# Mixture-of-experts stage: ranked experts, shared passes and plain f32 products on column groups

## The reference, cut to what matters

```python
N_GROUPS, EXPERTS_PER_GROUP, TOP_K, D_EXPERT = 4, 8, 2, 512      # 32 experts
lg = t @ w_router_group + b_router_group
g_sel = argmax(lg); g_w = softmax(lg)[g_sel]
le_sel = (t @ w_router_expert + b_router_expert)[g_sel]           # 8 logits of that group
top_v, top_i = top_k(le_sel, 2)
w_pair = g_w * softmax(top_v); e_id = g_sel * 8 + top_i
# for every expert e, over the rows routed to it:
hb = silu(xb @ w1[e]) * (xb @ w3[e])      # w1, w3: 1024 x 512
y  = (hb @ w2[e]) * w_b                    # w2: 512 x 1024
```

## Time and profile before

| | us |
|---|---|
| timed runs, median of 3 (lowest, highest) | 1218.3 (1218.05, 1220.96) |
| the profiled execution, by its span | 1219.4 |
| TensorE busy | 1147.7 (94%) |
| VectorE busy | 842.4 (69%) |
| ScalarE busy | 686.2 (56%) |
| GpSimd busy | 305.2 (25%) |
| DMA, mean over the span | 247 GB/s |

### The profile page before, as it was taken

The page is one execution under the profiler, slowest core; times in us unless marked ns, Lnnn a source line. Parts: engine busy times, 40 slices in busy tenths (PEclk is TensorE's granted clock), DMA queues, the critical chain, the costliest instruction groups (busy, mean ns, idle before and its releaser), DMA issues. The chain is left out here.

```text
span 1219.4 us, 16721 instructions
## 1 busy us (share of the span) xinstructions
PE 1147.7 (94%) x5993; PEld 921.9 (76%) x5993; DVE 842.4 (69%) x882; ACT 686.2 (56%) x799; POOL 305.2 (25%) x304
## 2 busy tenths in 40 slices
PE   4999999999888989999499999999999999999996
PEld 2677787777676878878478888888888888888873
DVE  3643232113688764616859999999999999999986
ACT  4332233223677541235257777787777777777754
POOL 1122131000113001002204334334433433443310
PEclk9999999999799999999789999999999999999988
DMA  9634534555501216421399999999999999999964
GB/s 357 216 132 147 140 124 157 181 181 181 200 1 38 85 45 234 136 70 35 134 361 384 386 377 378 380 368 370 360 372 362 362 369 368 367 363 371 363 254 172
DMA packets 151017, 301.30 MB, mean 247 GB/s; under 512 B 12031, under 2 KB 18304, under 8 KB 150322
## 3 DMA queue, kind: packets, MB, share of 16 engines
q1 hardware_dynamic: 135792, 271.07, 61.8%
q0 software_dynamic: 15008, 29.47, 7.3%
q10 hardware_dynamic: 162, 0.05, 0.0%
HBM read 290.68 MB, written 32.67 MB: 265 GB/s over the span
## 5 line engine op out<-in xcount | busy, mean ns | idle before, releaser
L1308 PE MATMUL psum<-w_hi,act_hi 128*128 128x512 f32 (+1 forms) x1248 | 497.8, 399 | 7.4 <-DVE act_lo L2205 2.4
L1310 PE MATMUL psum<-w_hi,act_lo 128*128 128x512 f32 (+1 forms) x1248 | 485.6, 389 | 0.0
L1309 PE MATMUL psum<-w_lo,act_hi 128*128 128x512 f32 (+1 forms) x1248 | 484.7, 388 | 0.0
L1308 PEld LDWEIGHTS psum<-w_hi,act_hi 128*128 128x128 f32 x1248 | 236.4, 189 | 71.4 <-issue 14.5
L1310 PEld LDWEIGHTS psum<-w_hi,act_lo 128*128 128x128 f32 x1248 | 236.2, 189 | 49.7
L1309 PEld LDWEIGHTS psum<-w_lo,act_hi 128*128 128x128 f32 x1248 | 236.8, 190 | 43.9
L2058 DVE TENSOR_TENSOR w_lo<-raw_extra,w_hi 128x2048 fp32r<-128x2048 f32 x96 | 217.2, 2290 | 35.2 <-ACT w_hi L1167 35.1
L2058 DVE TENSOR_TENSOR w_lo<-raw_mix,w_hi 128x2048 fp32r<-128x2048 f32 x96 | 219.7, 2288 | 13.4 <-ACT w_hi L1167 12.3
L1167 ACT ACTIVATE w_hi<-raw_mix 128x2048 fp32r<-128x2048 f32 x96 | 183.9, 1916 | 46.0 <-PE psum L1310 37.3
L1167 ACT ACTIVATE w_hi<-raw_extra 128x2048 fp32r<-128x2048 f32 x96 | 182.6, 1913 | 7.0 <-PE psum L1310 6.7
L1767 DVE TENSOR_TENSOR w_lo<-raw_mix,w_hi 128x2048 fp32r<-128x2048 f32 (+1 forms) x24 | 52.8, 2202 | 147.3 <-ACT w_hi L959 147.3
(11 more groups left out here) (308 smaller groups left out, 1265.6 us busy)
## 6 DMA issues: line engine op xcount, KB each, us to landing
raw_mix<-in_w_e SPq DMA_DIRECT2D x96, 1024.0 KB, 9.5
raw_extra<-in_w_e SPq DMA_DIRECT2D x96, 1024.0 KB, 9.6
raw_mix<-in_w_in SPq DMA_DIRECT2D x16, 1024.0 KB, 5.6
raw_mix<-in_w_ada SPq DMA_DIRECT2D x16, 1024.0 KB, 7.0
ada_first<-in_w_ada SPq DMA_DIRECT2D x8, 1024.0 KB, 14.4
gates_scratch<-rows POOLq DMA_DIRECT2D x20, 256.0 KB, 3.2
y_scratch<-lam SPq DMA_DIRECT2D x1, 5120.0 KB, 16.8
yrow<-gates_scratch POOLq DMA_DIRECT2D x20, 256.0 KB, 4.3
```

What stands on the lines that cost most here:

```text
L1308: pe.matmul(out, a_hi(ka_), w_hi[:, kw, :], start=s, stop=False)
L1309: pe.matmul(out, a_hi(ka_), w_lo[:, kw, :], start=False, stop=False)
L1310: ins = pe.matmul(out, a_lo(ka_), w_hi[:, kw, :], start=False, stop=e)
```

## The change

Three experts (numbers 0 to 2) and the last one (31) have fixed places. The 28 between are ranked by row count on the chip: VectorE compares each count with all others, TensorE turns the ranks into expert numbers and per-pass tables, and SyncE loads each expert number into a register ahead of its weight loads. `WIDTHS` lists 20 passes of 128 rows: 8 with one expert (three first, the four largest ranked, the last) and 12 with two of 64 rows each. Further rounds run if a count passes its place.

The split is gone from the experts. A step is two plain f32 products with 64 stationary columns, on column groups 0 to 63 and 64 to 127 of the same bank; in a pass of two experts each group has its own weights, in a pass of one both have the same. Weight loads go to 15 slots (`ring`): the three of `raw_mix`, the six of the then unused `w_hi` and `w_lo`, six over the attention rows. The k index is taken as partition-major (k = 8p + j), so that a partition's part of a unit is one run of 8 KB in DRAM (4 rows of 2 KB before); the transposes read the gathered rows at a stride of 8, the gated product at a stride of 4. A slot is free when its unit's products are done. GpSimd no longer copies table columns. The code for further rounds is new and is left out below.

```diff
-RAW_MIX, RAW_MOE, HL = 3, 6, 3
+RAW_MIX, RING, HL = 3, 15, 3
...
+LEAD, ALONE, QUADS = 3, 4, 0
+PAIRS = (NE - LEAD - 1 - ALONE - 4 * QUADS) // 2
+RANKED = NE - LEAD - 1
+WIDTHS = [1, 1, 1, 2, 2, 1, 2, 2, 2, 2, 2, 1, 2, 2, 1, 2, 1, 2, 2, 1]
...
+            first, step = {1: (0, ALONE), 2: (ALONE, PAIRS), 4: (ALONE + 2 * PAIRS, QUADS)}[n]
+            passes.append([("rank", first + x * step + i) for x in range(n)])
...
+    units = [(0, 1, 0), (0, 1, 1)]
+    for p in range(len(passes)):
+        units += [(p, 3, 0), (p, 3, 1)]
+        if p + 1 < len(passes):
+            units += [(p + 1, 1, 0), (p + 1, 1, 1)]
+        units += [(p, 2, 0), (p, 2, 1)]
+    loads = [(n, p, m, u, x) for n, (p, m, u) in enumerate(units) for x in range(len(passes[p]))]
...
-        w1 = t["w_e1"].rearrange("l e (k p) n -> (l e) p k n", p=P)
-        w3 = t["w_e3"].rearrange("l e (k p) n -> (l e) p k n", p=P)
-        w2 = t["w_e2"].rearrange("l e (k p) n -> (l e) p k n", p=P)
+        w_e = {1: t["w_e1"].rearrange("l e (p k) n -> (l e) p (k n)", p=P),
+               3: t["w_e3"].rearrange("l e (p k) n -> (l e) p (k n)", p=P),
+               2: t["w_e2"].rearrange("l e (p k) n -> (l e) p (k n)", p=P)}
...
+                _, p, m, u, x = moe_loads[j]
+                e = expert_number(*passes[p][x])
+                if j >= RING:
+                    sp.wait_ge(moe_mm, moe_loads[j - RING][0] + 1)
+                sp.dma_start(ring(j % RING), w_e[m][e][:, u * UNIT:(u + 1) * UNIT]).then_inc(raw_in[j % RING], 16)
...
+                for x in range(HL):
+                    sp.wait_ge(tile_mm, 5 * (NS - HL + x + 1))
+                    ring_load(RAW_MIX + 2 * x)
+                    ring_load(RAW_MIX + 2 * x + 1)
...
+                sp.wait_ge(h2_out, 16 * NT)
+                sp.wait_ge(h2t_done, 2 * NT)
+                for j in range(RAW_MIX + 2 * HL, len(moe_loads)):
+                    if j == RAW_MIX + 2 * HL + 4:
+                        sp.wait_ge(moe_g[0], 16)
+                    if j == RING - 1:
+                        sp.wait_ge(rt_mm, 1 + NT)
+                    ring_load(j)
...
+                if p >= 2:
+                    po.wait_ge(moe_xt, p - 1)
+                if p == LEAD:
+                    po.wait_ge(pass_done, 3)
...
+            for p in range(NP - 1):
+                if p + 2 < NP:
+                    gather(p + 2)
+                scatter(p)
...
+            def x_columns_copied(p):
+                par = p % 2
+                ac.wait_ge(moe_xt, p + 1)
+                ac.activation(expert_xT[:, par * D:(par + 1) * D], bank(0, 2), ACT.Copy).then_inc(moe_xc, 1)
...
+            pe.wait_ge(ranks_made, 2)
+            pe.matmul(bank(6)[0:1, 2 * NE:2 * NE + RANKED], tokval[0:NE, 0:1], perm[0:NE, :], start=True, stop=True)
+            pe.matmul(bank(6)[:, 0:2 * NE], ones_row[0:NE, :], excess[0:NE, :], start=True, stop=True).then_inc(ids_mm, 1)
...
+            xg_v = xg[:, :].rearrange("p (b q k) -> p b k q", b=2, k=KD)
+            gp_v = gprod[:, :].rearrange("p (q k) -> p k q", k=4)
...
+            def up_half(out, u, par, slots):
+
+                n = max(2, len(slots))
+                w = P // n
+                for kk in range(4):
+                    k = 4 * u + kk
+                    for x in range(n):
+                        a = par * D + k * P + x * w
+                        ins = pe.matmul(out[x * w:(x + 1) * w, :], expert_xT[:, a:a + w], ring(slots[x % len(slots)])[:, kk * 512:(kk + 1) * 512],
+                                        start=(k == 0), stop=(k == KD - 1))
+                return ins
+
+            def down_half(u, slots):
+                n = max(2, len(slots))
+                w = P // n
+                for kk in range(2):
+                    k = 2 * u + kk
+                    for b_ in range(2):
+                        for x in range(n):
+                            ins = pe.matmul(bank(5 + b_)[x * w:(x + 1) * w, :], gT[:, k * P + x * w:k * P + (x + 1) * w],
+                                            ring(slots[x % len(slots)])[:, kk * D + b_ * 512:kk * D + b_ * 512 + 512], start=(k == 0), stop=(k == 3))
+                return ins
...
+                    j = load_no[p, m, u, x]
+                    pe.wait_ge(raw_in[j % RING], landed(j))
+                    slots.append(j % RING)
...
+            for p in range(NP):
+                if p + 1 < NP:
+                    transpose_x(p + 1)
+                if p:
+                    pe.wait_ge(moe_gp, p)
+                up(p, 3, 0)
+                up(p, 3, 1)
+                if p + 1 < NP:
+                    pe.wait_ge(moe_si, p + 1)
+                    pe.wait_ge(moe_xc, p + 2)
+                    up(p + 1, 1, 0)
+                pe.wait_ge(moe_gp, p + 1)
+                if p:
+                    pe.wait_ge(moe_gc, p)
+                g_transposed().then_inc(moe_gt, 1)
+                if p + 1 < NP:
+                    up(p + 1, 1, 1)
+                pe.wait_ge(moe_gc, p + 1)
+                if p:
+                    pe.wait_ge(moe_ya, p)
+                    pe.wait_ge(moe_yv, p)
+                down(p, 0)
+                down(p, 1)
...
+            link(ve.scalar_tensor_tensor(key, counts, float(NE), order_bias[0:NE, :], ALU.mult, ALU.add))
+            link(ve.tensor_tensor(dg, key, on_diag, ALU.mult))
+            link(ve.tensor_reduce(small[:, 0:1], dg, AX.X, ALU.add))
+            link(ve.tensor_scalar(key, key, small[:, 0:1], None, ALU.is_gt))
+            link(ve.tensor_reduce(rank, key, AX.X, ALU.add))
+            link(ve.tensor_scalar(perm[0:NE, :], iota32[0:NE, 0:RANKED], rank, None, ALU.is_equal))
...
+            def gated_g(p):
+                ve.wait_ge(moe_mm, unit_end(p, 3, 1))
+                ve.wait_ge(moe_si, p + 1)
+                if p:
+                    ve.wait_ge(moe_gt, p)
+                ve.tensor_tensor(gprod[:, :], bank(3), gsil[:, :], ALU.mult).then_inc(moe_gp, 1)
+
+            def g_columns(p):
+                ve.wait_ge(moe_gt, p + 1)
+                ve.tensor_copy(gT[:, :], bank(4)).then_inc(moe_gc, 1)
```

More of the change, by code:

```diff
@@ L2276, in _ @@
             with ve.If(most > P):
[L2277 to L2287 removed]
+                later_round(1)
+                for r in range(2, ROUNDS):
+                    with ve.If(most > P * r):
+                        later_round(r)
                 for i in range(NT):
```

629 lines of the change are left out of this document (323 added, 306 removed).

## The result

The changed kernel takes 1152.6 us (median of 4 runs, 1152.25 to 1153.11), the kernel before in the same session 1218.6 us (1218.05 to 1220.96): ratio 0.9453, 95% interval 0.9439 to 0.9466, so 5.5% faster. The forecast was 1135 us with a range of 1108 to 1180: inside the range, 17.6 us above the forecast. The profiled execution has a span of 1150.5 us.

The account below looks back on a forecast made before the run. TensorE bounds the kernel before, DMA after: last piece of pass 18 lands at 1088.8 us, its last unit ends at 1092.2, pass 19 at 1108.5, tail 27.4 gives 1135.9, less 1.1: 1135 us; range 1108 to 1180.

Parts of the forecast that it names:

- What bounds the kernel before: Expert stage before the change: TensorE sets the pace at 17.8 us an expert; DMA follows at 14.8 us.
- The step of 0.86 us: Expert products: each k step of two 64-column f32 products costs 0.86 us, 20.6 us for a pass's 24 steps.
- Strided transposes at nothing: Transposes reading rows at a stride of eight: no extra cost taken, from a possible 0 to 1.15 us a pass.
- The first product: Start of the expert stage after routing: TensorE transposes at 610.0 us, first product at 613.3, before 614.58.
- Length of the rows: Weight loads: 8 KB rows move at 426 GB/s, so a bare 1.05 MB piece takes 2.46 us.
- The rival's 2.83: Weight loads, rival at 12%: longer rows bring nothing, a piece stays at 2.83 us with row traffic inside; 1173 us.
- Idle time of DMA in the leading passes: Passes 0 to 2 and first units of pass 3: DMA waits for slots to come free, 18.6 us.
- piece 187: Last weight piece that pass 18 needs: forecast to land at 1088.8 us, after 173 pieces of 2.59 us.
- The piece with its row traffic: Weight loads: gathers and scatters add 0.13 us to each 2.46 us piece, giving 2.59 us.
- The tail: From the last products' end to the end of the span: unchanged at 27.4 us.
- the forecast's own range: Total time by the forecast alone (69%): 1113 us at 2.46 us a piece, 1147 at 2.66 with a longer switch.
- two rivals: Longer rows bring nothing (12%, 1173 us); TensorE's step is longer than 0.86 us (13%, 1155 to 1160 us).

Follow-up runs that it names:

- e8: Kernel before the change, with w1 and w3 pieces read in rows of 8 KB, w2 unchanged, outputs wrong: 1218.4 us, ratio 0.9983.
- e4: Changed kernel with all k steps of column group 0 queued before those of group 1 in each unit, instead of alternating: 1174.3 us.
- e5: Changed kernel, but passes of one expert make one 128-column product a step instead of two of 64 columns: 1152.5 us.
- e1: Changed kernel with the weight layout of the kernel before (2 KB rows for w1 and w3, w2 in halves) and transposes on contiguous columns: 1185.6 us.
- e3: Changed kernel without three quarters of the w1 and w3 products and half of the w2 ones, loads and waits kept, outputs wrong: 1134.4 us (one run).
- e7: Changed kernel with gathers and scatters of passes 2 to 18 cut to one 4 KB row each, waits kept, outputs wrong: 1126.3 us.
- e9: Changed kernel with an expert's row positions spread over the partitions (position 8b + a of each 64 to partition 8a + b): 1163.5 us.
- e10: Changed kernel with another order of row positions, first 16 on partitions 0, 2, .. 14, 17, 19, .. 31: 1151.2 us, not told apart from the changed kernel.
- e2: Changed kernel with 11 weight slots instead of 15: 1162.7 us, ratio 0.9531.

## Why the prediction was right, and where it was off

1. *What bounds the kernel before.* Right: long rows alone change nothing there (e8).
2. *The step of 0.86 us.* Right to 1%: four steps take 3.49 us, 0.87 each. Without the alternation of the groups it would have been 1.02 us (e4), and at full width it is the same (e5).
3. *Strided transposes at nothing.* Nearly right. Eight take 1.08 us from start to start, 0.79 before, four take 0.68, before 0.36: 0.6 us a pass more. But e1's contiguous ones take 1.02 and 0.58, so the stride is 0.16 us of it; the rest comes with the new products around them, by a cause that isn't shown (in e5, strided but beside full-width products, they take 0.89 and 0.47). A pass is 22.67 instead of 22.1 us: 24 x 0.87 of steps, in which the changes of form are contained, and 1.76 of transposes. It cost little of the time, since DMA sets the end.
4. *The first product.* Forecast 613.3, measured 610.7: the gather went out at 602.3, and the transposes started at 607.6, 2.4 us before the forecast.
5. *Length of the rows.* Right: forecast 2.46 us for the bare piece from a row of 426 GB/s; the rate is 421, 2.49. The rival's 2.83 with row traffic inside is what short rows give: (1.0486 + 0.0506 MB) / 384 GB/s = 2.86 us (e1).
6. *Idle time of DMA in the leading passes.* Forecast 18.6 us. Measured: 60 us at 293 of 421 GB/s leave 18.2, 20 us at 402 leave 0.9. Taking it away let piece 187 be used 16.7 us sooner (e3).
7. *The piece with its row traffic.* This is the term that was mis-sized. From the first dynamic piece (616.1 + 1.3 = 617.4) to the landing of piece 187 (1102.5 - 1.2 = 1101.3) lie 483.9 us; less 19.1 of idle time, 464.8 for 173 pieces: 2.69 us, where the forecast had 2.59. That is 16.7 us more in all; with 0.5 more of idle time and a start 3.5 us earlier (617.4 for 620.9) it makes the 13.7 us between 1088.8 and 1102.5. The mean load of the engines explains 2.62: 419 GB/s over 700 to 1080 us is 2.50 a piece, and the 8.75 MB that e7 took out, over 173 pieces, another 0.12. The other 0.07 us, 12 us in all, is what is left over; I take it for the slowest engine behind the mean. e7 puts what the rows cost beyond their bytes lower, at some 7 us, so this size is uncertain. The step that failed is "Gathers and scatters move 2 x 1280 rows of 4 KB = 10.5 MB in the stage, 0.13 us a piece": it spreads them evenly over 16 engines, and each piece waits for the one that has most. That the row traffic does it is shown (e7), and that its place matters (e9). That e10 didn't even it out fits the rule of fours, by which its order leaves 240 row transfers on one engine where the mean is 156; an order even by that rule remains to be run.
8. *The tail.* Forecast 27.4 us, measured 1150.5 - 1122.3 (the last products' end, before VectorE's copy at 1122.50) = 28.2. TensorE's waits for slots: forecast 48 us, measured 42 (14.9 + 9.6 + 8.1 + 5.3 + 3.1 + 1.3).
9. *From the profile to the median.* I took off 1.1 us; this time the profiled execution lay 2.1 us below the median: 3.2 us of the miss.

13.7 + 0.8 + 3.2 = 17.7, the miss.

The mechanism was as forecast, but the forecast's own range, 1113 to 1147 us, doesn't hold 1152.6. The stated range does because it was widened for two rivals, and neither of them came true: longer rows brought 33 us, and the step was 0.87 us. So that the time lies inside it is in part luck.

Of the 66 us gained, e1 shows 33 for the longer rows and 33 for the rest, in which 15 slots instead of 11 are 10 (e2). What is left over TensorE's products is DMA: without three quarters of the w1 and w3 products and half of the w2 ones the kernel gets only 18 us faster.

## What to carry to other kernels

When a change turns a TensorE-bound stage into a DMA-bound one, price the slowest DMA engine, not the mean: look whether the rate ends sharply or fades. With a deep queue of pieces the rate stays near full (415 GB/s of 421 here) while every piece lands late by the lag of the slowest engine; only the end shows it. Before the limit moved, long rows were worth nothing; after it they were worth half of the gain, so edits of this kind have to be tried together.

## What the runs showed of the hardware that I had not expected

- The rate of weight pieces of 1.05 MB: rows of 8 KB 421 GB/s, rows of 2 KB 388 GB/s, on the same queue and beside the same row traffic. With the former a piece takes 27.6 us (median) from issue to landing, with the latter 14.3.
- The DMA engines of one core finish the same series of pieces up to 20 us apart when gathers and scatters of rows run beside it, 5 us apart without.
- Plain f32 products on two column groups overlap even when queued in blocks of four a group (1.02 against 0.86 us a step).
- f32 transposes of 128 x 128 took 0.135 us each at a stride of eight elements where contiguous ones took 0.13 beside the same products, and 0.17 at a stride of four where contiguous ones took 0.145. Beside the products of the kernel before they took 0.10 and 0.09: the neighbours matter more than the stride.
- The row transfers of a gather or scatter are tied to DMA engines by the partition: four engines were late in e9, eight in e10.
